# Moving the first context scores of a diffusion trunk's attention into the block substitution, the border tile's root ahead of a sum, and a gate behind the place sums

## The reference

```
h = modulate(rms_norm(x), shift, scale)              # shift, scale, gates from c @ ada_w
zq, zk, zv, zqkv, zg, zb, za = split(h @ w_in)       # 1024 -> 3600
o_na = softmax(q k^T + bias) v                       # 8 heads of 64; context sees context,
                                                     # latent sees a window and 128 cached keys
o_g  = gated delta rule, forward and backward        # 4 heads of 128, chunked, needs the inverse
                                                     # of a unit triangular matrix per chunk and head
x = x + g1 * (concat(o_na, norm(o_g) * silu(zg)) @ w_out)
x = x + g2 * moe(modulate(rms_norm(x)))              # 16 experts, 2 per token, 1024 -> 512 -> 1024
```

## Time and profile before

| | |
|---|---|
| median of 3 runs | 1420.54 us (1417.68 to 1421.13) |
| the profiled execution, its own time | 1427.51 us |
| its span, first to last instruction | 1425.7 us |
| PE busy | 1260.2 us, 88% of the span |
| DVE busy | 558.8 us, 39% |
| ACT busy | 307.3 us, 22% |
| POOL busy | 92.1 us, 6% |
| mean granted TensorE clock | 0.937 |
| DMA | 341.90 MB, mean 240 GB/s |

### The profile page before, as it was taken

The page is one execution under the profiler, slowest core; times in us unless marked ns, Lnnn a source line. Parts: engine busy times, 40 slices in busy tenths (PEclk is TensorE's granted clock), DMA queues, the critical chain, the costliest instruction groups (busy, mean ns, idle before and its releaser), DMA issues.

```text
span 1425.7 us, 21105 instructions
## 1 busy us (share of the span) xinstructions
PE 1260.2 (88%) x8895; PEld 622.7 (44%) x8895; DVE 558.8 (39%) x1446; ACT 307.3 (22%) x739; POOL 92.1 (6%) x104
## 2 busy tenths in 40 slices
PE   3999997899979898999949999869798898989893
PEld 0565544575553333333236654447556332333331
DVE  0245976563461121111242687836526221211113
ACT  1237412223121101010012661223312100101000
POOL 0010011000010000000021000020000100000001
PEclk8899998899989999999978999979998899999997
DMA  9810144778547999999981013355564599999994
GB/s 340 251 60 0 60 148 123 259 251 322 209 149 269 371 381 392 377 386 382 337 256 60 1 60 81 128 153 201 195 260 163 181 332 388 381 379 390 387 367 164
DMA packets 172977, 341.90 MB, mean 240 GB/s; under 512 B 34495, under 2 KB 36935, under 8 KB 172871
## 3 DMA queue, kind: packets, MB, share of 16 engines
q1 hardware_dynamic: 165095, 313.87, 61.9%
q0 software_dynamic: 7776, 26.55, 5.2%
HBM read 318.64 MB, written 21.76 MB: 239 GB/s over the span
## 4 chain that ended last, share of the span: by engine, by line
PE 67%; DMA 14%; DVE 13%; SPq 2%; issue 2%; ACT 1%; POOL 0%; DVEq 0%; POOLq 0%; ACTq 0%
PE bank L505 64%; DMA arena<-in_moe_w_dram 8%; PE bank L508 3%; DVE arena L1616 3%; DVE ring L1616 3%; DMA ring<-in_ada_w_dram 3%; DVE arena L1624 1%; DVE small L1624 1%; DMA arena<-expert_dram,idx_row 1%; SPq L1209 1%; DVE x L1624 1%; ACT arena L1312 1%; DMA arena<-tok_dram,idx 1%; DMA expert_dram<-arena 0%; DVE ring L1624 0%
## 5 line engine op out<-in xcount | busy, mean ns | idle before, releaser
L505 PE MATMUL bank<-ring,arena 128*32 128x512 f32 (+1 forms) x3952 | 531.7, 594 | 30.5 <-DMA arena<-in_moe_w_dram 15.9
L1312 ACT ACTIVATE arena<-bank 128x512 f32<-128x512 f32 (+3 forms) x344 | 156.9, 487 | 841.7 <-PE bank L505 458.6
L505 PEld LDWEIGHTS bank<-ring,arena 128*32 128x32 f32 (+1 forms) x3952 | 167.3, 114 | 321.1 <-issue 321.1
L505 PE MATMUL bank<-arena 128*32 128x512 f32 (+4 forms) x1296 | 243.6, 493 | 29.4 <-DVE arena L1616 22.2
L505 PE MATMUL bank<-ring,hT 128*128 128x512 f32 x576 | 253.9, 596 | 0.0
L1616 DVE TENSOR_TENSOR arena<-arena,bank 128x512 f32<-128x512 f32 x32 | 21.6, 686 | 395.0 <-PE bank L505 395.0
L505 PEld LDWEIGHTS bank<-ring,hT 128*128 128x128 f32 x576 | 108.1, 192 | 125.7 <-issue 125.2
L505 PE MATMUL bank<-hT,ring 128*128 128x384 f32 x384 | 133.0, 503 | 0.1
L505 PEld LDWEIGHTS bank<-arena 128*32 128x32 f32 (+3 forms) x1296 | 92.7, 140 | 91.9 <-issue 53.6
L1616 DVE TENSOR_TENSOR arena<-bank,arena 128x512 f32<-128x512 f32 x60 | 41.5, 692 | 149.2 <-PE bank L505 149.2
L505 PEld LDWEIGHTS bank<-hT,ring 128*128 128x128 f32 x384 | 74.0, 197 | 48.8 <-issue 4.8
(11 more groups left out here) (128 smaller groups left out, 794.6 us busy)
## 6 DMA issues: line engine op xcount, KB each, us to landing
ring<-in_moe_w_dram SPq DMA_DIRECT2D x80, 2048.0 KB, 13.9
ring<-in_ada_w_dram SPq DMA_DIRECT2D x24, 2048.0 KB, 8.6
arena<-in_moe_w_dram SPq DMA_DIRECT2D x16, 2048.0 KB, 16.2
ring<-in_w_in_dram SPq DMA_DIRECT2D x14, 2048.0 KB, 10.0
expert_dram<-arena SPq DMA_DIRECT2D x24, 512.0 KB
ring<-in_w_out_dram SPq DMA_DIRECT2D x4, 2048.0 KB, 9.1
arena<-in_na_rpb_dram SPq DMA_DIRECT2D x32, 96.0 KB, 4.4
tok_dram<-arena POOLq DMA_DIRECT2D x6, 512.0 KB, 3.0
```

The lines of the kernel that those rows point to most:

```text
L505: return nc.tensor.matmul(out, lhsT, rhs, start=start, stop=stop)
L1312: return nc.scalar.activation(out, in_, func, **kw)
```

## The change

Three edits, in both layers.

1. Context scores. `scores(0)` is issued right behind `token_major(2, 1)`, into banks 7 and 3, which are free there, with semaphores of its own (`first_full`, `first_taken`). `probs_cols(0)` and `scores(1)` follow `token_major(2, 2)`. On ScalarE `probs(0)` goes between `token_tile(2, 1)` and `qk_cols(1, 1)`, and `probs_T(0)`, `probs(1)` ahead of `qk_cols(1, 2)`. On VectorE `maxima(0)`, `turns(0)` and `maxima(1)` go between the steps of the substitution, behind j = 10, 7 and 3; the norms move from behind j = 30, 18 and 8 to 30, 20 and 13. `RULE_AT` goes from 4 to 5: each rule piece falls half a step later.
2. At the head of layer 1 `token_scale(l, 1, 0)` comes before `combined(l - 1, 1)`.
3. `gate_rows(2, (1,))` goes behind the place and count sums; the lists use banks 7 and 6 in the other order, and the wait for all ScalarE jobs moves from ahead of the lists to ahead of their second group.

```diff
-RULE_AT = 4
+RULE_AT = 5
...
                 token_major(2, 1)
+                pe.wait_ge(act_emptied, job["qkT", l, 1, 0])
+                pe.wait_ge(ada_taken, jobs["ada"] // SHARE)
+                if l:
+                    pe.wait_ge(x_ready, 6 * l)
+                scores(0)
                 qk_cols(1, 1)
                 token_major(2, 2)
+                probs_cols(0)
+                scores(1)
                 qk_cols(1, 2)
...
                 pe.wait_ge(act_emptied, job["past", l])
-                scores(0)
                 for step in range(N_STEPS):
-                    probs_cols(step)
-                    if step + 1 < N_STEPS:
-                        scores(step + 1)
+                    if step:
+                        probs_cols(step)
+                        if step + 1 < N_STEPS:
+                            scores(step + 1)
                     rule(2 * step - RULE_AT)
...
                     if t == 2:
                         token_rows(2)
-                        gate_rows(2, (1,))
                         pe.wait_ge(routed, TILES * l + 3)
...
                     last = mm(b[:, 0:16], ones, chosen[:, s, :], s == 0, s == TILES - 1)
                 last.then_inc(for_dve, 1)
+                gate_rows(2, (1,))
...
                         pe.wait_ge(s["sel"], g + 1)
+                        if s is es and group == 1:
+                            pe.wait_ge(act_emptied, jobs["act"])
...
-                                last = mm(bank[6 + group % 2][:, 2 * c_:2 * c_ + 2], sel[group % 2][:, t, c_ * P:(c_ + 1) * P],
+                                last = mm(bank[7 - group % 2][:, 2 * c_:2 * c_ + 2], sel[group % 2][:, t, c_ * P:(c_ + 1) * P],
...
-                pe.wait_ge(act_emptied, jobs["act"])
                 lists(es, l * EXPERTS)
...
                 token_tile(2, 1)
+                probs(0)
                 qk_cols(1, 1)
                 token_tile(2, 2)
+                probs_T(0)
+                probs(1)
                 qk_cols(1, 2)
...
                 if l:
                     combined(l - 1, 0)
+                token_scale(l, 1, 0)
+                if l:
                     combined(l - 1, 1)
-                token_scale(l, 1, 0)
...
+                def between(j):
+
+                    if j in (30, 20, 13):
+                        qk_norm(3 + (30, 20, 13).index(j))
+                    elif j == 10:
+                        maxima(0)
+                    elif j == 7:
+                        turns(0)
+                    elif j == 3:
+                        maxima(1)
...
-                        if j in (BLOCK - 2, BLOCK - 14, BLOCK // 2 - 8):
-                            qk_norm(3 + (BLOCK - 2, BLOCK - 14, BLOCK // 2 - 8).index(j))
+                        between(j)
...
-                maxima(0)
-                turns(0)
+                turns(1)
                 for step in range(N_STEPS):
-                    if step + 1 < N_STEPS:
+                    if step and step + 1 < N_STEPS:
                         maxima(step + 1)
```

More of the change, by code:

```diff
@@ L694, in head_products @@
                         last.then_inc(for_dve, 1)
[L696 to L724, removed]
                 def scores(step):
@@ L729, in scores @@
                     keys = slice(0, P) if t == 0 else slice(P, 512)
-                    todo = [(act_bank("score", l, no), heads_) for no, heads_ in jobs_of(step)]
+                    todo = [(bank[(7, 3)[no]] if step == 0 else act_bank("score", l, no), heads_) for no, heads_ in jobs_of(step)]
                     for j in range(len(todo[0][1])):
@@ L737, in scores @@
                             if h == heads_[-1]:
-                                last.then_inc(for_act, 1)
+                                last.then_inc(for_act if step else first_full, 1)
                 def probs_cols(step):
@@ L1515, in rule @@
                             mixed_T("og", t, 4)
-                probs(0)
                 for step in range(N_STEPS):
-                    probs_T(step)
-                    if step + 1 < N_STEPS:
-                        probs(step + 1)
+                    if step:
+                        probs_T(step)
+                        if step + 1 < N_STEPS:
+                            probs(step + 1)
                     rule(2 * step - RULE_AT)
@@ L1851, in head_products, with maxima @@
                     ts(n_exp[:, :, GH * t:GH * t + GH], gexp[:, :, 0, GH * t:GH * t + GH], -1.0).then_inc(raw_ready, 1)
+                def maxima(step):
+                    t, h0, n_heads = STEPS[step]
+                    for no, heads_ in jobs_of(step):
+                        if step:
+                            dve.wait_ge(for_act, job["score", l, no])
+                            b = bank[4 + (job["score", l, no] - 1) % 3]
+                        else:
+                            dve.wait_ge(first_full, 2 * l + no + 1)
+                            b = bank[(7, 3)[no]]
+                        if t == 0:
+                            vec.tensor_reduce(neg_max[:, 0, heads_.start:heads_.stop:2],
+                                              b[:, 0:2 * P].rearrange("p (h n) -> p h n", h=2),
+                                              AX, ALU.max, negate=True).then_inc(s_ready, 1)
+                        else:
+                            h = heads_[0]
+                            if h % 4 == 0:
+                                dve.wait_ge(bias_ready, 2 * l + h // 4 + 1)
+                            r0 = BIAS_ROWS - ROWS if t == 1 else 0
+                            link(tt(b[:, 0:LAT], b[:, 0:LAT], flat(bias[h // 4][:, h % 4, r0:r0 + ROWS, :]), ALU.add))
+                            vec.tensor_reduce(neg_max[:, t, h:h + 1], b[:, 0:LAT + PAST], AX, ALU.max,
+                                              negate=True).then_inc(s_ready, 1)
@@ new lines, in turns @@
+                def turns(step):
+                    t, h0, n_heads = STEPS[step]
+                    if step:
+                        dve.wait_ge(act_emptied, job["score", l, jobs_of(step)[-1][0]])
+                    else:
+                        dve.wait_ge(first_taken, 2 * l + 2)
+                    sums = row_sum[:, t, h0:h0 + n_heads]
+                    link(vec.reciprocal(sums, sums))
+                    if t == 0:
+                        tt(turn_b, heads(ident, 2), over(sums[:, 2:4], P))
+                    tt(turn_a, heads(tab("flip") if t else ident, 2), over(sums[:, 0:2], P)).then_inc(turn_ready, 1)
```

99 lines of the change are left out of this document (51 added, 48 removed).

## The result

The changed kernel takes 1438.53 us (median of 4 runs, 1434.64 to 1443.97) against 1419.82 (4 runs, 1417.68 to 1421.13): a ratio of 1.0136 [1.0100, 1.0172], 19 us slower. Its profiled execution took 1434.64 us, with a span of 1432.8, a mean granted clock of 0.943 and PE busy 1260.4 us: TensorE does the same work at the same mean clock and sits idle longer. The profiled execution of before lies 7.7 us over its median, so the two spans differ by 7.1 us only. For stages I therefore set several profiles beside each other.

What follows compares the result with a forecast made beforehand. It took the kernel as mostly TensorE-bound, with TensorE partly idle early in each mixing stage. Layer 0 +6.1 and layer 1 -11.8 gave -5.7 us, from the median 1420.54 to 1414.8, rounded 1415; range 1408 to 1425.

Steps and rivals of the forecast that it cites:

- rival D: Whole kernel: VectorE stalls in the substitution, solved comes 3.6 + 7 us late, +5 us, 1426; chance 0.18.
- signs of being wrong: Forecast is wrong if layer 0's slab isn't later, or layer 1's rule pieces wait over 6 us in all.
- net +1.2: Layer 0, after the third slab: piece 1 undone adds 3.2 us, piece 10 falling behind the load returns 2.0.
- Piece 2 waits for VectorE's five copies ...: 1.0: Layer 1's rule pieces: TensorE's piece 2 waits 1.0 us for five VectorE copies, 2.8 us behind maxima(4).
- edit 3's -3.7: Gate row moved behind the place sums: -1.4 us in layer 0 and -2.3 in layer 1.
- The substitution: Both layers: 2.5 us of added work plus waits of 0.4 and 0.7 make solved 3.6 us later.
- The third slab: Layer 0: SyncE's path to the slab load moves 2.7 us later, ends 1.5 and 3.6; fourth slab doesn't slow it.
- The end of layer 0: ScalarE's squares queue behind probs(9), so og comes 16.1 us after the load: net +3.6 us, ends 1 and 6.
- Layer 1's head: Layer 1's mixing: attention starts earlier, less later substitution and piece waits: gain of 5.5 us, ends 2 and 8.
- the 2.0 of its end: End of layer 1's mixing: work moves into the wait ahead of og, gate rows start 2.0 us earlier, ends 0 and 4.
- Rival C: Layer 1's gain is eaten by rule pieces waiting on each other, 6 us, its end worth nothing: 1419; chance 0.27.
- Edit 2: Head of layer 1: the root waits only for ScalarE's squares, so 2.0 us earlier, ends -2.4 and -1.

Runs made afterwards that it cites:

- e9: Changed kernel with RULE_AT 5 in layer 0 only, 4 in layer 1: 1428.11 us, ratio 1.0031 to the kernel before.
- e2: Changed kernel with RULE_AT back at 4, everything else of the change kept: 1415.72 us, ratio 0.9956 to the kernel before.
- e5: Kernel before with RULE_AT 5 and nothing else: 1437.80 us, ratio 1.0115 to the kernel before.
- e7: Changed kernel with rule pieces 0 to 3 back at their old half steps: 1421.18 us, ratio 1.0016 to the kernel before.
- e10: Changed kernel with only rule pieces 0 and 1 back at their old half steps: 1424.70 us, ratio 1.0009 to the kernel before.
- e6: Changed kernel with rule pieces 11 to 13 back at their old half steps: 1432.65 us, ratio 1.0078 to the kernel before.
- e8: Changed kernel with RULE_AT 4 and the second gate row, list banks and wait put back: 1412.69 us, ratio 0.9950 to the kernel before.
- e11: Early scores alone on the kernel before, RULE_AT 4, without the other two edits: 1416.30 us, ratio 0.9945 to the kernel before.
- e12: e8 with the last tile's key columns, bias rows and mask moved earlier: 1422.73 us, ratio 0.9983 to the kernel before.
- e4: Kernel before with only the moved token_scale and the moved gate row, no early scores: 1420.47 us, ratio 0.9988 to the kernel before.

## Why the prediction was wrong

The forecast was 1415 us, the result 1438.5, outside the range; rival D named a slower kernel, but at 1426 and by a stall of the substitution that is not there. Both of its own signs of being wrong came: layer 0's slab was not later, and layer 1's rule pieces waited over 6 us. **The step that failed is the one on the rule pieces: "net +1.2" in layer 0, and "Piece 2 waits for VectorE's five copies ...: 1.0" in layer 1.** In layer 0 the load behind them moved by 5.9 us, all of it from there; in layer 1 TensorE waited 6.28 us for those copies. In layer 0 I had given RULE_AT 5 1.2 us here and 3.6 at the end, 4.8 in all; e9 and e2, which have it there and not, differ by 10.7 in that stage. Run alone it costs 16 us (e5), undone in the changed kernel it gives 23 (e2). The second term that failed is edit 3's -3.7, of which nothing came. Point by point:

**The substitution**, forecast +3.6 us, measured +2.3 (40.1 us from its first copy's start to its last copy's end, against 37.8). The two waits in it (0.4 and 0.7) are not there. VectorE in layer 0 (in time):

```profile
226.81 0.76 DVE L1875 TENSOR_REDUCE small<-bank 128x2 f32<-128x256 f32 x2
...
229.78 0.18 DVE L1894 RECIPROCAL small<-small 128x4 f32<-128x4 f32 x1
...
234.82 1.07 DVE L1926 COPY ring<-ring 112x1024 f32<-112x1024 f32 x1
...
236.01 0.42 DVE L1627 TENSOR_TENSOR ring<-const,small 128x256 f32<-128x256 f32 x1
```

From `maxima(0)` to the reciprocal it is 2.97 us, with three steps between (2.26 us) and no wait; ScalarE's table load of 1.28 us, part of the 3.34 I had reckoned with, now runs at 222.05 while ScalarE waits for VectorE.

**The third slab**, forecast 2.7 us later, was issued 0.2 us earlier (252.22 against 252.40), although `solved` came 1.7 us later (235.89 against 234.23). SyncE's queue:

```profile
235.91 2.78 SPq L1202 DMA_DIRECT2D inv_dram<-ring  x4
241.80 3.91 SPq L1208 DMA_DIRECT2D ring<-inv_dram  x8
...
252.22 2.94 SPq L1217 DMA_DIRECT2D ring<-in_ada_w_dram  x2
```

The read-back began only 1.0 us later (before at 240.76), and its eight issues took 3.91 us in place of 5.13. In the earlier trace rows the wait for the write was part of the chain; it is so still. The fourth slab followed sooner, as foreseen, and did not slow the third, for which I had put nothing: TensorE could start on the third slab 12.2 us after its issue, where it had been 12.4. The chain leads through the slab as I said, and that TensorE would idle "10 us or more" ahead of it was right (14.08).

**Piece 1 and piece 10**, forecast net +1.2. The load that stood at 324.41 was issued at 330.30: +5.9, all of it from here, since the slab gave none. In the rows above piece 1 took 5.8 us from 271.26 to 277.03, of which 3.68 are the gap; the product behind it lost 1.5 (3.40 against 1.92), and nothing of this had cover. The direction was right: I had piece 1 leave the wait and put its whole time on the path. The price was wrong, 3.2 us where the piece and the product cost 7.3. My 3.2 to 4.0 came from layer 1, where piece 1 had a gap of 1.55 us, and the slow product behind it was in no term of layer 0; piece 10 gave back the 2.0 that I had for it. What I did not ask is what piece 1 would be worth at its old place, ahead of a wait that I had just forecast at 10 us or more. e2, e7 and e10 show it: with piece 1 inside the wait, TensorE gets from the slab's product to the columns in 7.7 to 10.0 us and not in 15.8.

**The end of layer 0**, mechanism right, size 1.9 us too small. I put `og` 16.1 us behind the load; it came 16.4 behind it (346.73). From `og` to the gate rows I had 5.7 us, and it took 7.3 (to 354.01), since the product after the wait ran at 3.17. ScalarE's squares in layer 1, behind the exponentials of step 9 as foreseen:

```profile
1024.68 0.30 ACT L1320 ACTIVATE arena<-arena 128x128 f32<-128x128 f32 x1
...
1027.22 0.84 ACT L1320 ACTIVATE arena<-bank 128x384 f32<-128x384 f32 x2
```

I had put their eight at 2.4 us; here they are 2.5. In layer 1 the wait was 4.18 us in place of 4.99. From the start of the last score columns to the gate rows it took 17.8 us, not 18.5, a gain of 0.7 where I had 2.0, and the gate rows then took 5.67 us, not 3.84, at a granted clock of 0.65 where it had been 1.00.

```profile
1031.28 1.12 PE L508 MATMUL bank<-const,arena 128*128 128x128 f32 x4 [4.18 <-DVE arena L1627]
...
1037.29 5.67 PE L505 MATMUL bank<-const,mod 128*128 128x128 f32 x32 [0.28 <-DVE mod L1627]
```

The sum for layer 0 as it came out: 5.9 + 4.2 + 1.3 = 11.4, and the gate rows moved from 342.56 to 354.01. e6, which takes the digit away from this end in both layers, wins 5 to 8 us by the ratios. Its profile shows less: from the slab's product to the gate rows 2.4 us in layer 0, and in layer 1 a mixing stage no shorter (146.5 us) with gate rows 1.8 us shorter.

**Layer 1's head**, forecast -5.5. The early gain came: `turns(1)` stands right behind `solved`, and in both layers its halves take 0.42 us, where the first of them took 0.97 in layer 0 and 1.70 in layer 1. With the pieces half a step late it was lost at the mask: attention reached step 4 before the mask did, whose place I had not moved in my sum, and piece 1's copies were queued behind it (6.28 and 1.85 us of waits where I had 3.6 in all). e2, e8 and e11, with the pieces at their old place, keep 6 to 8 us of it. The stage gave 0 to 3 us where, with the 2.0 of its end, 7.5 were forecast. Rival C had this kind of loss but not its size: I had the pair waits as matmul and copy latencies, and looked for no DMA in them.

The Trainium skill's rule (SBUF — State Buffer, Who interferes with whom), by which the bias add is not slowed by GpSimd, agrees with this trace: GpSimd scales from 945.14 to 947.20, above, and VectorE's add that begins at 945.37 took 0.42 us.

**Edit 2**, forecast -2.0. Tile 0's `combined` ends at 738.59, the squares take 1.22 us, the root 2.3:

```profile
735.99 2.60 DVE L1635 SCALAR_TENSOR_TENSOR x<-arena,small,x 128x1024 f32<-128x1024 f32 x2 [11.03 <-DMA arena<-expert_dram,idx_row]
739.81 0.34 DVE L1631 TENSOR_SCALAR small<-small 128x1 f32<-128x1 f32 x2 [1.22 <-ACT arena L1320]
```

```profile
742.07 3.14 PE L505 MATMUL bank<-arena,x 128*128 128x128 f32 x13 [17.85 <-DVE arena L1632]
```

(The last row is cut off by the end of its view.) The stage got 2.4 us shorter; it took 12.6 to 13.2 us in the ten profiles with the edit and 14.5 to 15.1 in the four without. The mechanism and the size are right; that the kernel got faster by it isn't shown (e11 against e8).

**Edit 3**, forecast -3.7, gave nothing that can be measured. From the gate rows to the first gather of tokens it was 71.1 us in layer 0 (before 70.9) and 73.3 in layer 1 (before 72.5). The gate row did only change its place in the same chain:

```profile
418.31 1.89 PE L505 MATMUL bank<-small,const 128*128 128x16 f32 x8 [1.75 <-DVE small L1627]
420.03 3.60 PE L505 MATMUL bank<-const,mod 128*128 128x128 f32 x16
```

```profile
418.95 0.21 DVE L1635 SCALAR_TENSOR_TENSOR small<-bank,small 128x48 f32<-128x48 f32 x1 [0.54 <-PE bank L505]
...
423.88 0.17 DVE L2138 COPY small<-bank 128x6 f32<-128x6 f32 x1 [1.30 <-PE bank L505]
```

The first half of the forecast came: VectorE waited 0.54 us for the place sums, where it had waited 1.81. But TensorE had waited 1.75 us for `routed` ahead of them, and the gate row behind ran slowly (3.60 us for 16 records, 2.44 before), so that the first list was late and VectorE waited 1.30 for it: what was won was lost again. I had said that VectorE reads the list "a selection later", and had taken the gate row at its full-clock price behind an idle TensorE.

What stays open: some 4 us of layer 1's loss that the medians have and neither its mixing nor its gate rows show (the two profiles of the changed kernel themselves differ by 3.7); and how much of the head's loss is the gap, how much the clock. No run took the one away without the other.

## What to carry to other kernels

Before moving work later by a step, look in the trace for the longest wait that stands next to it, and ask on which side of that wait the work will lie; an in-order engine hides nothing that is queued behind the wait. If two things are moved in one edit, price each as if it were alone, also the one that looks like bookkeeping: here the early scores give 0.5% by themselves (1416.3 us against 1424.8), and the digit that came with them takes back some three times that. When attention is made to run ahead, check everything it will meet sooner, transfers above all (the bias rows). And moving those transfers ahead in an issuing queue delays every store behind them (e12).

## What the runs showed of the hardware

A run of over a hundred small matmuls behind a long wait can stop for 3.6 to 4.0 us. It did in layer 0 of all six profiles in which piece 1 lay behind the slab, each time after 138 records (gaps of 3.68, 3.85, 3.71, 3.92, 3.98 and 3.59 us), and in none of e2, e7, e8, e10 and e11, where it ran in one go before the slab landed. (In e12 too it ran in one go.) A long wait in front isn't needed for a gap: in the kernel before and in e4, whose piece 1 is at its old place too, it lies after 43 records and took 1.23 and 2.88 us, and in layer 1 of e10 it took 1.97. It isn't a wait for a bank: piece 1 takes its two banks ahead of its first and its 97th record. The DMA view of the changed kernel from 274 to 275 us has this row (queue, packets, MB, share of the engines):

```profile
q8 instruction: 1, 0.02, 7.0%
```

It is one packet on the instruction queue, some two microseconds ahead of TensorE's restart at 276.61. In each of the other five such a packet lies some 2 to 3 us ahead of the restart as well, and from 254 to 274 the changed kernel has none. In the kernel before and in e4 it lies 2 to 3 us ahead of the restart too (259 to 260 and 260 to 261 us, restarts at 262.12 and 262.97). In e2, e7, e8, e10 and e11 it lies between 259 and 262 us, inside the wait for the slab. So I take the gap for a wait for instructions; which engine a packet is for isn't recorded, so this is argued and not shown.

The Trainium skill (Runtime: NRT & Kernel Launch, Instruction fetch mechanics) says that TensorE's instruction memory is refilled in blocks of 16 KiB by DMA and that this is mostly hidden. The packet's size fits (0.02 MB). If the gap is such a refill, it was not hidden here, by 3.68 us.

The slab's product ran at the lower of the two clock levels, 1.2 GHz: the granted clock was 0.50 from 264.46 to 268.03, after 14.08 us of idle time, and the product took 3.64 us against 1.92 at 2.4 GHz. The length of the wait doesn't tell it: in the kernel before, after 1.34 us (and a gap of 1.23 just ahead), it was 0.50 too and the product took 3.64. What the clock cost the changed kernel beyond the kernel before is mainly the 1.5 us in the product behind the gap (0.55 from 276.95 to 280.30). At the two ends it cost both of them much the same, at different places: in layer 0 the product behind `og` took 3.17 us, where before the one at 332.40 had taken 3.40, behind a wait of 2.88; in layer 1 the gate rows lost 1.8, where before the product behind `og` had lost 1.6 (3.49).
